# Feed-forward of a transformer block: gate and up products by seven 256-token blocks (Strassen) in place of eight, weight sums on GpSimd, down products a phase later

## The chip, the cores and the metric

The kernel runs on one core of a Trainium2 chip. The time is device time in microseconds of one launch, the median of several runs. A core has TensorE (PE in the profile), VectorE (DVE), ScalarE (ACT), GpSimd (POOL) and SyncE (SP), which issues the loads. Each engine works through its own queue in order; engines wait for each other on semaphores only.

## The reference

Two blocks of a language model in float32 over 512 tokens of width 1024. The first has two layers (a recurrent mixer and a sparse attention), each followed by the same feed-forward; the second has a retention and window attention mixer and a mixture of experts. Only the feed-forward matters here. It runs twice:

```python
D_FF = -(-8 * D_MODEL // (3 * 256)) * 256          # 2816

def swiglu(h, w_gu, w_down):
    u = h @ w_gu
    g, v = u[..., :D_FF], u[..., D_FF:]
    return (jax.nn.silu(g) * v) @ w_down
...
        h = h + swiglu(rmsnorm(h, norm_g[layer, 1]), ffn_w_gu[layer], ffn_w_down[layer])
```

## The kernel before

Float32 products are made of three matmuls each: every operand is split into a rounded part `hi` (ACT, a copy with another type) and the rest `lo` (DVE, a subtraction), and `three` multiplies hi by hi, hi by lo and lo by hi into one PSUM bank.

The hidden width 2816 is cut into 22 tiles of 128. Tokens are the moving operand. For one tile, `linear` makes the gate product into `bank[2v]` and the up product into `bank[2v+1]` (v is the tile's parity), each over eight slices of the model width, with 512 tokens at a time: 2 x 8 x 3 = 48 matmuls. The normalization's factor per token (`rn`) is multiplied in afterwards, twice on DVE (before and after the silu on ACT); DVE then multiplies gate by up into `hid`, ACT and DVE split it. `down` takes two hidden tiles (f = 0, 1) at once: for each half of the model width (hb = 0, 1) four output tiles into banks 4 to 7, first the four products of f = 0, then the four of f = 1, 48 matmuls in all. DVE's `add_y` adds each bank into `h`; a bank's first product of the next half waits for that add (`y_free`).

A pair of tiles is one trip of a hardware loop on each engine: on TensorE `linear`, `linear`, `down`. The order of the work on DVE and ACT is written out by hand in `ffn_pair` (lines near 1690 and 2390). Weight panels of 1 MB (gate and up columns of a tile) come into `a_raw[0]` and `a_raw[1]` in turn. SP's `load_a` (near line 535) waits for `a_ready` to show that DVE's `low_a` of the tile two before is done, as that is the last reader of the buffer. `load_b` does the same for the down weights, and both are issued from one queue in the order a0, b0, a1, b1. GpSimd does nothing in the feed-forward but sums of squares ahead of it.

## Time and profile before

| | us |
|---|---|
| median of 3 runs | 2142.63 |
| lowest and highest | 2141.57, 2142.84 |
| the profiled execution, from first to last instruction (span) | 2139.6 |
| TensorE busy | 2097.5 (98%) |
| DVE busy | 1267.3 (59%) |
| ACT busy | 836.2 (39%) |
| GpSimd busy | 270.8 (13%) |

The span is the profiled execution's own time between its first and last instruction. What a run takes outside it is not in the profile; the median of the runs is 3.0 us above the span. Busy times of an engine are the union of its instructions; matmuls overlap each other, so the time between two starts says more than the duration of one. The first feed-forward takes about 240 to 610 us of the span, the second about 1040 to 1400 us.

### The profile page before, as it was taken

To read this page: it belongs to the slowest core of one execution; us is meant where nothing else is said; L and a number is where in the kernel's file an instruction comes from. 1 tells how busy PE (TensorE), PEld (TensorE's weight loads), DVE (VectorE), ACT (ScalarE), POOL (GpSimd) and SP (SyncE) were. 2 spreads that over 40 slices of the span, in tenths; PEclk is the share of its full clock that TensorE was granted. 3 is DMA by queue.
4 is the path that set the end of the run, shared out by engine and by line. 5 is a ranking of instruction groups with operands and counts; after the bars stand their busy time and mean duration, and the time that the engine had idled before them with its cause. 6 is when DMAs were issued, how large, how long until landed. Compare 5 with 4: busy or idle time off the path is not lost.

```text
span 2139.6 us, 27223 instructions
## 1 busy us (share of the span) xinstructions
PE 2097.5 (98%) x10474; PEld 1579.8 (74%) x10474; DVE 1267.3 (59%) x1704; ACT 836.2 (39%) x1258; POOL 270.8 (13%) x234
## 2 busy tenths in 40 slices
PE   8999999999999999999999999999999999999998
PEld 6787788888878877888888888877778884333346
DVE  7887855554587678875655555488775454000038
ACT  6556522222253444774422222264542232222143
POOL 1334200000010064000100000020000023222220
PEclk9999999999999999999999999999999999999999
DMA  5322322223214352122322222212122158999961
GB/s 202 125 94 74 118 92 105 88 88 117 79 64 147 130 172 79 31 46 90 131 91 99 104 88 88 98 61 78 60 99 98 62 239 321 418 408 401 391 238 60
DMA packets 62622, 298.13 MB, mean 139 GB/s; under 512 B 14080, under 2 KB 14464, under 8 KB 34582
## 3 DMA queue, kind: packets, MB, share of 16 engines
q1 hardware_dynamic: 42560, 261.60, 32.0%
q0 software_dynamic: 19552, 34.55, 5.3%
q8 instruction: 63, 1.03, 0.2%
q10 hardware_dynamic: 416, 0.70, 0.1%
q14 instruction: 31, 0.25, 0.0%
HBM read 326.37 MB, written 22.48 MB: 163 GB/s over the span
## 4 chain that ended last, share of the span: by engine, by line
PE 80%; DVE 8%; DMA 5%; ACT 3%; issue 2%; POOL 1%; POOLq 0%; ACTq 0%; DVEq 0%
PE psum L652 21%; PE psum L654 21%; PE psum L653 21%; PE psum L1413 5%; PE psum L1437 3%; DMA panel<-w_m 3%; PE psum L1102 2%; PE psum L1077 1%; DVE a_lo L2137 1%; DMA over_panel<-w_m,over_row 1%; ACT a_hi L1520 1%; DVE xc L2294 1%; DVE hs L2248 1%; ACT hn_hi L1547 0%; PE psum L1235 0%
## 5 line engine op out<-in xcount | busy, mean ns | idle before, releaser
L652 PE MATMUL psum<-hn_hi,a_hi 128*128 128x512 f32 (+1 forms) x1592 | 628.2, 395 | 1.9 <-DVE a_lo L2126 0.9
L654 PE MATMUL psum<-hn_hi,a_lo 128*128 128x512 f32 (+1 forms) x1592 | 618.5, 389 | 0.0
L653 PE MATMUL psum<-hn_lo,a_hi 128*128 128x512 f32 (+1 forms) x1592 | 618.1, 388 | 0.0
L652 PEld LDWEIGHTS psum<-hn_hi,a_hi 128*128 128x128 f32 (+1 forms) x1592 | 297.0, 187 | 73.5 <-issue 7.8
L653 PEld LDWEIGHTS psum<-hn_lo,a_hi 128*128 128x128 f32 (+1 forms) x1592 | 297.1, 187 | 64.8 <-issue 2.4
L654 PEld LDWEIGHTS psum<-hn_hi,a_lo 128*128 128x128 f32 (+1 forms) x1592 | 297.0, 187 | 64.4
L2137 DVE TENSOR_TENSOR a_lo<-a_raw,a_hi 128x2048 fp32r<-128x2048 f32 (+2 forms) x108 | 247.2, 2289 | 69.6 <-ACT a_hi L1520 69.1
L1520 ACT ACTIVATE a_hi<-a_raw 128x2048 fp32r<-128x2048 f32 (+2 forms) x108 | 201.3, 1866 | 71.2 <-PE psum L654 62.0
L2236 DVE TENSOR_TENSOR h<-h,psum 128x512 f32<-128x512 f32 x176 | 119.4, 686 | 78.4 <-PE psum L654 78.4
L3150 POOL TENSOR_TENSOR sq<-sq 128x512 f32<-128x512 f32 x5 | 7.8, 1555 | 1118.2 <-ACT sq L1533 1118.2
L3072 DVE TENSOR_TENSOR xhid<-xsg,psum 128x256 f32<-128x256 f32 x24 | 10.1, 421 | 232.3 <-ACT xsg L2081 232.3
L1701 ACT ACTIVATE sg<-sg 128x512 f32<-128x512 f32 x44 | 27.8, 632 | 286.2 <-DVE sg L2407 286.2
L652 PE MATMUL psum<-hid_hi,b_hi 128*128 128x512 f32 x352 | 137.3, 390 | 2.1 <-DVE h L2236 2.0
L654 PE MATMUL psum<-hid_hi,b_lo 128*128 128x512 f32 x352 | 137.0, 389 | 0.0
L653 PE MATMUL psum<-hid_lo,b_hi 128*128 128x512 f32 x352 | 136.9, 389 | 0.0
L1413 PE MATMUL psum<-panel,xw 128*64 128x512 f32 x512 | 113.4, 595 | 0.0
L2412 DVE TENSOR_TENSOR hid<-sg,psum 128x512 f32<-128x512 f32 x44 | 30.3, 688 | 113.8 <-PE psum L654 113.7
L1703 ACT ACTIVATE hid_hi<-hid 128x512 fp32r<-128x512 f32 x44 | 27.8, 632 | 177.5 <-DVE hid L2412 177.5
L1527 ACT ACTIVATE b_hi<-b_raw 128x1024 fp32r<-128x1024 f32 x64 | 66.9, 1050 | 65.5 <-PE psum L654 63.2
L1413 PEld LDWEIGHTS psum<-panel,xw 128*64 128x64 f32 x512 | 35.4, 137 | 66.8 <-issue 66.5
L2143 DVE TENSOR_TENSOR b_lo<-b_raw,b_hi 128x1024 fp32r<-128x1024 f32 x64 | 79.7, 1252 | 1.0 <-ACT b_hi L1527 1.0
L652 PEld LDWEIGHTS psum<-hid_hi,b_hi 128*128 128x128 f32 x352 | 66.1, 188 | 17.4 <-issue 2.6
(533 smaller groups left out, 3261.2 us busy)
## 6 DMA issues: line engine op xcount, KB each, us to landing
a_raw<-w_a SPq DMA_DIRECT2D x115, 1024.0 KB, 5.0
panel<-w_m SPq DMA_DIRECT2D x96, 1024.0 KB
b_raw<-w_b SPq DMA_DIRECT2D x64, 512.0 KB, 3.4
q_scratch<-q_hi POOLq DMA_DIRECT2D x7, 384.0 KB
q_scratch<-qb_lo POOLq DMA_DIRECT2D x7, 384.0 KB
q_hi<-q_scratch POOLq DMA_DIRECT2D x7, 384.0 KB
q_lo<-q_scratch POOLq DMA_DIRECT2D x7, 384.0 KB
token_rows<-nat POOLq DMA_DIRECT2D x4, 512.0 KB, 5.5
```

The costliest lines, as they stand in the source:

```text
L652: pe.matmul(out, w_hi, x_hi, start=first, stop=False)
L653: pe.matmul(out, w_hi, x_lo, start=False, stop=False)
L654: return pe.matmul(out, w_lo, x_hi, start=False, stop=last)
L1102: mm = pe.matmul(bank[6 + at % 2][side * DV:(side + 1) * DV, t * P:(t + 1) * P], w, x, start=i == 0, stop=i == len(steps) - 1)
L1413: mm = pe.matmul(bank[v][rows, :], xw[:, v, k, rows], w[half][:, k % 4 * 2 * EFF:(k % 4 + 1) * 2 * EFF], start=k == 0, stop=k == KT - 1)
L1437: mm = pe.matmul(bank[4 + 2 * v + hb][rows, :], xturn[:, v, f * P + half * SLOTS:f * P + (half + 1) * SLOTS], w[half][:, f * D + hb * 512: ...
L1520: act.activation(a_hi[s % 2][:, 0:w], a_raw[s % 2][:, 0:w], ACT.Copy).then_inc(a_rounded, 1)
L1527: act.activation(b_hi[s % 2][:, :], b_raw[s % 2][:, :], ACT.Copy).then_inc(b_rounded, 1)
L2137: V.tensor_tensor(a_lo[s % 2][:, 0:w], a_raw[s % 2][:, 0:w], a_hi[s % 2][:, 0:w], ALU.subtract) \
L2143: V.tensor_tensor(b_lo[s % 2][:, :], b_raw[s % 2][:, :], b_hi[s % 2][:, :], ALU.subtract) \
L2236: V.tensor_tensor(h[:, m, :], h[:, m, :], bank[4 + m % 4][:, :], ALU.add).then_inc(y_free, 1)
L2412: V.tensor_tensor(hid[:, f, :], sg[:, f, :], ps[1][:, :], ALU.mult).then_inc(tile_free, 2)
```

## The change

For 20 of a feed-forward's 22 tiles (all but the first two) gate and up are made together as a 2 by 2 block product by Strassen's method in Winograd's form. The blocks are: the two halves of the model width (four slices each), gate or up columns, and tokens 0 to 255 or 256 to 511. Seven block products of 4 slices x 3 matmuls with 256 columns take the place of eight: `P_1, P_2, P_6, P_7, P_5` in the tile's own phase, `P_3` and `P_4` in the phase of the tile after. Each has its own weight slot (`slot_hi`, `slot_lo`), one buffer each.

Four weight sums a tile (`S_1` to `S_4`, 128x512) and the second scaling of the gate are made on GpSimd, which holds them in one buffer `wsum`. Four token transforms (`T1` to `T4`, of the normalized input with its gain, for each of four slices) are made once in front, on ACT, GpSimd, ACT and DVE. Partial results are copied from PSUM by ACT (`copy_1` to `copy_3`) and added by DVE (`add_11`, `add_21`, `add_22`). The splitting of a tile's weights, one 2048-wide instruction on ACT and one on DVE before, becomes five on each: `high_1`/`low_1` and `high_s23`/`low_s23` 1024 wide, `s1`, `s4` and `a22` 512 wide. `a_ready` is now counted up by `low_a22`. SP's code is unchanged. `down` of a pair stands between the two phases of the next pair, and the loop's bounds change with it. The tables `rel` and `dk`, loaded by GpSimd ahead of the second feed-forward before, are loaded behind it.

The core of the diff, in the order TensorE, ACT, DVE, GpSimd (what is left out are index helpers, buffer declarations and the small functions whose names say what they read, round or add):

```diff
+            def seven(out, slot, x_hi, x_lo, again=False):
+                for k in range(KT // 2):
+                    mm = three(out, slot_hi[:, slot, k, :], slot_lo[:, slot, k, :], x_hi(k), x_lo(k),
+                               not again and k == 0, k == KT // 2 - 1, again)
+                return mm
+            def tx(n):
+                return lambda k: tx_hi[:, k, n, :], lambda k: tx_lo[:, k, n, :]
+            def hn_block(k0, c):
+                return lambda k: hn_hi[:, k0 + k, c], lambda k: hn_lo[:, k0 + k, c]
+            def fast_phase(sa, g, i, v):
+                n, m = sa + v + 2 * i, v - 2 + 2 * i
+                first = isinstance(i, int) and m == 0
+                x, z, y = bank[2 * v][:, 0:HALF], bank[2 * v + 1][:, 0:HALF], bank[2 * v + 1][:, HALF:S]
+                split, copied = split_at(g) + 4 * m, copied_at(g) + 3 * m
+                pe.wait_ge(tile_free, 2 * n - 2)
+                pe.wait_ge(w_split, split + 1)
+                seven(x, P_1, *hn_block(0, slice(0, HALF))).then_inc(w_used, 1)
+                seven(y, P_2, *hn_block(KT // 2, slice(0, HALF))).then_inc(w_used, 1)
+                if not first:
+                    pe.wait_ge(part_copied, copied)
+                    pe.wait_ge(w_split, split + 2)
+                    seven(bank[2 - 2 * v][:, 0:HALF], P_3, *hn_block(KT // 2, slice(HALF, S)), again=True) \
+                        .then_inc(w_used, 1)
+                else:
+                    pe.wait_ge(tx_ready, tx_at(g + 1))
+                pe.wait_ge(part_copied, copied + 1)
+                pe.wait_ge(w_split, split + 3)
+                seven(x, P_6, *tx(T2), again=True).then_inc(w_used, 2 if first else 1)
+                if not first:
+                    pe.wait_ge(a_ready, n)
+                    pe.wait_ge(part_added, added_at(g) + 2 * m)
+                    seven(bank[3 - 2 * v][:, 0:HALF], P_4, *tx(T4), again=True).then_inc(tile_ready, 2)
+                pe.wait_ge(part_added, added_at(g) + 2 * m + 1)
+                seven(z, P_7, *tx(T3)).then_inc(w_used, 1)
+                pe.wait_ge(part_copied, copied + 2)
+                pe.wait_ge(w_split, split + 4)
+                seven(x, P_5, *tx(T1), again=True).then_inc(w_used, 1)
...
+            def ffn(sa, sb_, e, trips, q, t, g):
                 linear_first(sa, q)
                 sums(t)
                 linear(sa + 1)
+                fast_phase(sa, g, 1, 0)
                 down(sb_, e, 0, hid_hi, hid_lo, P)
-                with pe.Fori(1, trips) as i:
-                    linear(sa, i)
-                    linear(sa + 1, i)
-                    down(sb_, e, i, hid_hi, hid_lo, P)
-
-            ffn(A_FF0, B_FF0, E_FF0, FF_TILES // 2, N_FFN0, T_FFN0)
+                fast_phase(sa, g, 1, 1)
+                with pe.Fori(2, trips) as i:
+                    fast_phase(sa, g, i, 0)
+                    down(sb_ - 2, e - 1, i, hid_hi, hid_lo, P)
+                    fast_phase(sa, g, i, 1)
+                fast_last(sa, g)
+                down(sb_, e, trips - 1, hid_hi, hid_lo, P)
...
+            def high_tx(g, k):
+                act.wait_ge(tx_made, tx_at(g, 4) + 4 * k + 4)
+                act.activation(tx_hi[:, k, :, :], tx_of(k), ACT.Copy).then_inc(tx_rounded, 1)
...
+            def first_pair(sa, sb_, e, t, g, gain):
+                gain_x(0, gain)
+                high_a(sa + 1)
+                gain_x(1, gain)
+                gain_x(2, gain)
+                high_tx(g, 0)
+                high_b(sb_)
+                act.wait_ge(tx_ready, tx_at(g) + 1)
+                gain_x(3, gain)
+                high_tx(g, 1)
+                high_b(sb_ + 1)
+                high_tx(g, 2)
+                root_wide(t)
+                high_1(sa, g, 1, 0)
+                high_tx(g, 3)
+                silu(e, 0, 0)
+                high_hid(0, tile_free, 2 * sa + 2)
+                high_s23(sa, g, 1, 0)
+                high_s1(sa, g, 1, 0)
+
+            def fast_pair(sa, sb_, e, i, g, last=False):
+                first = isinstance(i, int) and i == 1
+                copy_1(g, i, 0)
+                high_1(sa, g, i, 1)
+                silu(e, i - 1, 1)
+                copy_2(sa, g, i, 0)
+                high_s4(g, 2 * i - 1)
+                high_hid(1, *((tile_free, 2 * sa + 4) if first else (hid_made, hid_at(g) - 2 + 2 * i)))
+                high_a22(sa, i, 0)
+                high_s23(sa, g, i, 1)
+                copy_3(g, i, 0)
+                high_s1(sa, g, i, 1)
+                high_b(sb_, i)
+                copy_1(g, i, 1)
+                high_b(sb_ + 1, i)
+                if not last:
+                    high_1(sa, g, i + 1, 0)
+                silu(e, i, 0)
+                copy_2(sa, g, i, 1)
+                high_s4(g, 2 * i)
+                high_hid(0, hid_made, hid_at(g) - 1 + 2 * i)
+                high_a22(sa, i, 1)
+                if not last:
+                    high_s23(sa, g, i + 1, 0)
+                copy_3(g, i, 1)
+                if not last:
+                    high_s1(sa, g, i + 1, 0)
+
+            def ffn(sa, sb_, e, trips, t, g, gain):
+                first_pair(sa, sb_, e, t, g, gain)
+                fast_pair(sa, sb_, e, 1, g)
+                with act.Fori(2, trips - 1) as i:
+                    fast_pair(sa, sb_, e, i, g)
+                fast_pair(sa, sb_, e, trips - 1, g, last=True)
+                act.wait_ge(w_used, used_at(g + 1) - 2)
...
+            def low_a22(n, v):
+                V.wait_ge(a_rounded, n + 1)
+                V.tensor_tensor(slot_lo[:, P_4, :, :], panel_view(v)[:, KT // 2:KT, 1, :], slot_hi[:, P_4, :, :], ALU.subtract) \
+                 .then_inc(a_ready, 1)
...
+            def first_pair(sa, sb_, e, t, g):
+                low_a(sa + 1)
+                low_tx(g, 0)
+                low_b(sb_)
+                low_tx(g, 1)
+                low_b(sb_ + 1)
+                low_tx(g, 2)
+                inverse_wide(t)
+                gate(e, sa, 0, 0)
+                low_1(g, 0, 0)
+                low_tx(g, 3)
+                hidden(e, sa, 0)
+                low_hid(e, 0, 0)
+                low_s23(g, 0, first=True)
+                gate(e, sa + 1, 0, 1)
+                low_s1(g, 0)
+
+            def fast_pair(sa, sb_, e, i, g, last=False):
+                first = isinstance(i, int) and i == 1
+                n, m = sa + 2 * i, 2 * i - 2
+                add_11(g, m, 0)
+                if first:
+                    hidden(e, sa + 1, 1)
+                low_1(g, m + 1, 1)
+                scale_11(g, m, 0)
+                if not first:
+                    scale_12(used_at(g) + 6 * m + 3, 1)
+                low_s4(split_at(g) + 4 * m + 6)
+                if not first:
+                    add_21(n - 1, 1)
+                    fast_hidden(e, n - 1, i - 1, 1)
+                low_hid(e, i - 1, 1)
+                low_a22(n, 0)
+                low_s23(g, m + 1)
+                add_22(g, m, 0)
+                low_s1(g, m + 1)
+                for k in range(4):
+                    add_y(sb_ - 2 + 2 * i, k)
+                low_b(sb_, i)
+                for k in range(4, KT):
+                    add_y(sb_ - 2 + 2 * i, k)
+                add_11(g, m + 1, 1)
+                low_b(sb_ + 1, i)
+                scale_11(g, m + 1, 1)
+                if not last:
+                    low_1(g, m + 2, 0)
+                scale_12(used_at(g) + 6 * m + 9, 0)
+                low_s4(split_at(g) + 4 * m + (9 if last else 10))
+                add_21(n, 0)
+                fast_hidden(e, n, i, 0)
+                low_hid(e, i, 0)
+                low_a22(n + 1, 1)
+                if not last:
+                    low_s23(g, m + 2)
+                add_22(g, m + 1, 1)
+                if not last:
+                    low_s1(g, m + 2)
...
+            def make_tx(g, k):
+                x, tx = x_of(k), tx_of(k)
+                b11, b12, b21, b22 = x[:, 0, 0:HALF], x[:, 0, HALF:S], x[:, 1, 0:HALF], x[:, 1, HALF:S]
+                pool.wait_ge(x_gained, gained_at(g) + 2 * k + 2)
+                pool.tensor_tensor(tx[:, T1, :], b12, b11, ALU.subtract).then_inc(tx_made, 1)
+                pool.tensor_tensor(tx[:, T3, :], b22, b12, ALU.subtract).then_inc(tx_made, 1)
+                pool.wait_ge(tx_made, tx_at(g, 4) + 4 * k + 1)
+                pool.tensor_tensor(tx[:, T2, :], b22, tx[:, T1, :], ALU.subtract).then_inc(tx_made, 1)
+                pool.wait_ge(tx_made, tx_at(g, 4) + 4 * k + 3)
+                pool.tensor_tensor(tx[:, T4, :], b21, tx[:, T2, :], ALU.subtract).then_inc(tx_made, 1)
+            def sum_three(sa, g, i, v):
+                m, first = v - 2 + 2 * i, isinstance(i, int) and v - 2 + 2 * i == 0
+                a, done = panel_view(v), summed_at(g) + 4 * m
+                pool.wait_ge(a_loaded[(sa + v) % 2], 16 * ((sa + v) // 2 + i) + 16)
+                if first:
+                    pool.wait_ge(tx_ready, tx_at(g + 1))
+                else:
+                    pool.wait_ge(w_split, split_at(g) + 4 * m)
+                pool.tensor_tensor(wsum[:, S_1, :, :], a[:, 0:4, 1, :], a[:, 4:8, 1, :], ALU.add).then_inc(w_summed, 1)
+                pool.tensor_tensor(wsum[:, S_3, :, :], a[:, 0:4, 0, :], a[:, 0:4, 1, :], ALU.subtract).then_inc(w_summed, 1)
+                pool.wait_ge(w_summed, done + 1)
+                pool.tensor_tensor(wsum[:, S_2, :, :], wsum[:, S_1, :, :], a[:, 0:4, 0, :], ALU.subtract) \
+                    .then_inc(w_summed, 1)
+            def sum_last(g, i, v):
+                m, first = v - 2 + 2 * i, isinstance(i, int) and v - 2 + 2 * i == 0
+                pool.wait_ge(w_summed, summed_at(g) + 4 * m + 3)
+                if not first:
+                    pool.wait_ge(w_split, split_at(g) + 4 * m + 2)
+                pool.tensor_tensor(wsum[:, S_4, :, :], panel_view(v)[:, 4:8, 0, :], wsum[:, S_2, :, :], ALU.subtract) \
+                    .then_inc(w_summed, 1)
+            def scale_gate(e, i, v):
+                pool.wait_ge(gate_done, 2 * (e - E_FF0 + i) + v + 1)
+                pool.tensor_tensor(sg[:, v, :], sg[:, v, :], rn[:, :], ALU.mult).then_inc(gate_scaled, 1)
+            def fast_pair(sa, e, i, g, last=False):
+                if not (isinstance(i, int) and i == 1):
+                    scale_gate(e, i - 1, 1)
+                sum_three(sa, g, i, 1)
+                sum_last(g, i, 1)
+                if not last:
+                    sum_three(sa, g, i + 1, 0)
+                scale_gate(e, i, 0)
+                if not last:
+                    sum_last(g, i + 1, 0)
+            def ffn(sa, e, trips, g):
+                for k in range(KT // 2):
+                    make_tx(g, k)
+                sum_three(sa, g, 1, 0)
+                sum_last(g, 1, 0)
+                fast_pair(sa, e, 1, g)
+                with pool.Fori(2, trips - 1) as i:
+                    fast_pair(sa, e, i, g)
+                fast_pair(sa, e, trips - 1, g, last=True)
+                scale_gate(e, trips - 1, 1)
```

## Rows read from the trace of the kernel before

**Rows 1.** The page: engine totals, and the chain of waits by engine.

```profile
PE 2097.5 (98%) x10474; PEld 1579.8 (74%) x10474; DVE 1267.3 (59%) x1704; ACT 836.2 (39%) x1258; POOL 270.8 (13%) x234
...
PE 80%; DVE 8%; DMA 5%; ACT 3%; issue 2%; POOL 1%; POOLq 0%; ACTq 0%; DVEq 0%
```

**Rows 2.** Busy time by engine in one pair and in nearly ten (us, instructions in brackets).

```profile
310.00:342.64 32.64, 32.64 (x145) 27.04 (x144) 17.65 (x20) 8.15 (x8) 0.00 (x0) 1.00 0.26 96
280.00:600.00 320.00, 320.00 (x1414) 265.05 (x1413) 173.01 (x195) 80.10 (x80) 0.00 (x0) 1.00 0.26 95
```

**Rows 3.** Timeline of TensorE, 512 columns (start us, us, engine, line).

```profile
317.72 0.39 PE L652 MATMUL psum<-hn_hi,a_hi 128*128 128x512 f32 x1
317.95 0.39 PE L653 MATMUL psum<-hn_lo,a_hi 128*128 128x512 f32 x1
...
318.85 0.39 PE L654 MATMUL psum<-hn_hi,a_lo 128*128 128x512 f32 x1
```

**Rows 4.** Timeline of TensorE, 256 columns, and a weight load there.

```profile
2125.26 0.28 PE L652 MATMUL psum<-hn_hi,a_hi 128*128 128x256 f32 x1
2125.38 0.28 PE L653 MATMUL psum<-hn_lo,a_hi 128*128 128x256 f32 x1
...
2125.26 0.19 PEld L653 LDWEIGHTS psum<-hn_lo,a_hi 128*128 128x128 f32 x1
```

**Rows 5.** Instructions by shape (busy us, mean ns); last GpSimd's min/median/max ns.

```profile
L3072 DVE TENSOR_TENSOR xhid<-xsg,psum 128x256 f32<-128x256 f32 x24 | 10.1, 421 | 232.3 <-ACT xsg L2081 232.3
L2414 DVE TENSOR_TENSOR hid_lo<-hid,hid_hi 128x512 fp32r<-128x512 f32 x44 | 30.5, 692 | 30.7 <-ACT hid_hi L1703 30.7
L2143 DVE TENSOR_TENSOR b_lo<-b_raw,b_hi 128x1024 fp32r<-128x1024 f32 x38 | 46.2, 1218 | 0.0
...
L2081 ACT ACTIVATE xsg<-psum 128x256 f32<-128x256 f32 x24 | 9.2, 384 | 139.6 <-PE psum L1413 133.4 <-issue 6.1
L1703 ACT ACTIVATE hid_hi<-hid 128x512 fp32r<-128x512 f32 x44 | 27.8, 632 | 177.5 <-DVE hid L2412 177.5
L1527 ACT ACTIVATE b_hi<-b_raw 128x1024 fp32r<-128x1024 f32 x64 | 66.9, 1050 | 65.5 <-PE psum L654 63.2 <-DMA b_raw<-w_b 2.2
...
L3150 POOL TENSOR_TENSOR sq<-sq,tmp x10: 1292/1558/3157, 242.4 to 1728.6; 128x512 f32<-128x512 f32 x10
```

**Rows 6.** Timelines of GpSimd and DVE where they overlap.

```profile
1717.40 2.40 POOL L3150 TENSOR_TENSOR sq<-sq 128x512 f32<-128x512 f32 x1 [302.26 <-ACT sq L1533]
1727.15 4.64 POOL L3150 TENSOR_TENSOR sq<-sq,tmp 128x512 f32<-128x512 f32 x2 [7.34 <-ACT tmp L1533]
...
1718.58 0.68 DVE L2681 TENSOR_TENSOR h<-h,psum 128x512 f32<-128x512 f32 x1
1727.25 3.39 DVE L2137 TENSOR_TENSOR a_lo<-a_raw,a_hi 128x2048 fp32r<-128x2048 f32 x1
```

**Rows 7.** Timeline of DVE in the feed-forward loop.

```profile
319.37 0.69 DVE L2407 TENSOR_TENSOR sg<-psum,rn 128x512 f32<-128x512 f32 x1 [1.50 <-PE psum L654]
320.76 0.69 DVE L2409 TENSOR_TENSOR sg<-sg,rn 128x512 f32<-128x512 f32 x1 [0.70 <-ACT sg L1701]
...
327.98 2.29 DVE L2137 TENSOR_TENSOR a_lo<-a_raw,a_hi 128x2048 fp32r<-128x2048 f32 x1 [1.11 <-ACT a_hi L1520]
```

**Rows 8.** DMA issues of the page: the panels (KB each, median us to landing).

```profile
a_raw<-w_a SPq DMA_DIRECT2D x115, 1024.0 KB, 5.0
```

**Rows 9.** Timelines around the first feed-forward's prologue.

```profile
258.94 3.35 DVE L2169 RECIPROCAL rn<-rn 128x512 f32<-128x512 f32 x1 [3.03 <-ACT rn L1544]
...
268.91 0.39 PE L652 MATMUL psum<-hid_hi,b_hi 128*128 128x512 f32 x1
```

**Rows 10.** Windows in the experts' stage; PEclk is the granted clock.

```profile
1894.00:1898.00 4.00, 3.18 (x8) 1.14 (x10) 0.43 (x1) 0.11 (x1) 0.00 (x0) 0.64 1.02 411
1940.00:1966.00 26.00, 25.13 (x118) 8.06 (x113) 2.55 (x6) 5.65 (x10) 6.03 (x6) 1.00 1.02 410
```

**Rows 11.** The chain that ended last, in order of time (start us, us, what).

```profile
1878.53 16.16 DMA panel<-w_m
```

More of the change, by code:

```diff
@@ L28 @@
 FF_TILES = 2816 // P
+HALF = S // 2
+T1, T2, T3, T4 = range(4)
+S_2, S_3, S_1, S_4 = range(4)
+P_1, P_2, P_6, P_7, P_5, P_3, P_4 = range(7)
+NFAST = FF_TILES - 2
 HEADS, GROUPS, DQK, DV = 16, 4, 96, 64
@@ L3171, in _ @@
             sums(T_FFN0)
+            ffn(A_FF0, E_FF0, FF_TILES // 2, 0)
             sums(T_KV)
```

265 lines of the change are left out of this document (194 added, 71 removed).

## The prediction

> **What bounds the kernel now.** I read the page's engine totals and chain first: TensorE is busy 98% of the span and four fifths of the chain of waits is TensorE [rows 1]. The stretch 280 to 600 us, nearly ten pairs of feed-forward tiles, has TensorE busy 320.00 of 320.00 us, DVE 173, ACT 80 and GpSimd nothing; one pair lasts 32.64 us and DVE works 17.65 of it [rows 2]. So here only fewer or shorter matmuls can gain, and other work is free as long as no matmul waits for it. The reader is to see how much room DVE has before and who will want it.
>
> **The products.** A matmul of 512 columns starts 0.2267 us after the one before it (317.72 to 317.95; over the pair's 144, 32.64 us) [rows 2, 3]. One of 256 columns, with the same kinds of operand, starts 0.12 us after (2125.26 to 2125.38), although a weight load lasts 0.19 us; the loads overlap [rows 4]. Gate and up of a tile are 2x8x3 = 48 matmuls now, 48 x 0.2267 = 10.88 us; seven products are 7x4x3 = 84, 84 x 0.12 = 10.08 us. That is 0.80 us a tile, 20 fast tiles in each of two feed-forwards: -32.0 us. A pair without any wait: 32.64 - 1.6 = 31.04 us, in the order first tile's phase A 0 to 10.08 (seven groups of 1.44: 1, 2, 3', 6, 4', 7, 5; a prime is the tile before), down products 10.08 to 20.96, phase B of the second tile 20.96 to 31.04.
>
> **What the other engines get.** Per tile, by width: DVE 256 wide x5 (0.42 us), 512 wide x5 (0.69), 1024 wide x3 (1.22, the old b_lo included), and four adds into h (0.69, as the other 512 wide) [rows 5]: 2.1 + 3.5 + 3.7 + 2.8 = 12.0 us, 24 us a pair where it was 17.65. Queued ones start 0.09 earlier, about 21 us. ACT: 3x0.38 + 5x0.63 + 3x1.05 = 7.4, 15 us a pair, no bound. GpSimd: four sums and the gate scaling, 5 a tile. Its 512-wide TENSOR_TENSOR takes 1.29 us at the least, 1.56 in the median, waits for DVE included [rows 5]: 12.9 us a pair. No row shows these sums' strided reading; I take 1.29, with 1.56 as upper end; as lower end the 0.69 of DVE's instruction of that width.
>
> **GpSimd beside DVE.** At 1727.15 GpSimd starts two 512-wide operations and at 1727.25 DVE a 2048-wide subtraction of two SBUF tensors. DVE takes 3.39 in place of 2.29 [rows 7], GpSimd 4.64 in place of 2.6: exactly what comes out if one waits for the other's whole instruction, GpSimd 1727.15 to 1728.45, DVE to 1730.64, GpSimd to 1731.8. At 1717.40 it is GpSimd that waits, 2.40 in all. The add from PSUM at 1718.58 takes 0.68 beside GpSimd's, undisturbed [rows 6]. Of the new DVE work only add_11, scale_12, add_21, add_22 and the h adds read PSUM. The rest, 9 instructions a tile, about 7.5 us, shares one turn with GpSimd's 6.5: 14 of the 15.5 us of a tile's share, and in turns.
> The Trainium skill, SBUF — State Buffer, "SBUF: two separate sides", says the same: an exclusive lock between GpSimd and a DVE instruction with two SBUF inputs, held for the whole instruction. By that rule, the trace agrees (3.39 against 2.29 us). A reader who took it as shared bandwidth would price case 2 below.
>
> **The queues, worked through for pairs 2 to 10.** Hops: a product's end reaches DVE or ACT 0.29 us after its last slot (last matmul 318.85, next slot 319.08, DVE 319.37); DVE to ACT to DVE costs 0.07 beside the work (319.37 to 320.76) [rows 3, 7]. A panel lands 5.0 us after its issue (median of 115) [rows 8], and SP issues about 0.15 after the DVE instruction that frees the buffer.
> Phase B, from its start: product 2 done 3.17; ACT's high_1 to 4.22; DVE low_b 3.5 to 4.7, scale_11, low_1 5.0 to 6.2, scale_12 to 6.5; silu to 7.2; GpSimd scale_gate 7.2 to 8.5; low_s4, which waits for it, to 9.2; GpSimd's last sum 9.2 to 10.5; fast_hidden to 11.2; high_hid to 11.85; low_hid to 12.5; low_a22 to 13.15. No matmul of phase B waits (copy_2 is done at 7.5, product 5 wants it at 8.64). But this runs 3.1 us into the next pair (t = 0 is its start), and four waits follow:
> (a) copy_3 stands in ACT's queue behind high_hid, high_a22 and high_s23: done t = 3.55, product 3' wants it at 2.88: **0.7 us**.
> (b) SP's load of the second tile's panel waits for a_ready, now given by low_a22 at 3.1: issued 3.25, landed 8.25. Behind it: high_1 to 9.35, low_1 to 10.6, scale_11, scale_12 to 11.3, silu to 11.95, copy_2 to 12.3 (ACT takes silu first). Product 5, due at 8.64 + 0.7, starts at 12.3: **2.95 us**. Before the change no product waits for a panel: TensorE has no gap in 320 us [rows 2].
> (c) GpSimd and DVE then take turns: scale_gate to 13.3, low_s4 14.0, sum 15.2, fast_hidden 15.9, sum 17.1, low_hid 17.8 (high_hid between). Down products begin at 13.8; four groups of the first hidden half cover 2.7 us, then they wait for low_hid: **1.3 us**.
> (d) low_s23 and low_s1 of the next tile stand before the eight h adds in DVE's queue, and low_s23 waits for GpSimd's third sum: sum 19.0, low_a22, last sum 20.9, low_s23 22.1 (high_s23 20.1), add_22, low_s1 23.0, first add into h 23.6. Down's second half wants the bank that this add frees at 20.6: **3.1 us**.
> 8.05 us a pair: 31.04 + 8.05 = 39.1 against 32.64, **+6.5 us** for each of 9 pairs: +58.5.
> **First pair and prologue:** -1.6 for the tiles. In front of it, ACT's root_wide (behind it now DVE's reciprocal from 258.94, 3.35 us, and the first down product at 268.91 [rows 9]) stands behind eight gains, three rounded transforms, and those behind 12 GpSimd operations of 256 columns. No row has that width: between half of 1.29 and 1.29; I take 0.75, 9 us, plus about 3 of turns with a_lo and b_lo. The reciprocal ends about 267.8, low_1 and low_tx go before hidden, the banks come free at about 271.6 where TensorE wants them at 268.9: 2.7. The first three weight sums start only when all transforms are split (270.6), low_s23 ends 277.2, product 6 wanted it 2.4 earlier; product 7 another 0.4. **+5.5** (bounds 1 to 12 by the two widths).
> **End:** after the last phase B product 3' wants copy_3 at once, 2.4 us early; then the last hidden half comes 0.8 after down's first half ends. **+3.2** (0 to 5).
> Code outside the loops (the two table loads moved behind the second feed-forward, used 50 us later) costs nothing.
>
> **Sum.** Per feed-forward 58.5 - 1.6 + 5.5 + 3.2 = 65.6; two: +131. The span is 2139.6 and the median of the runs lies 3.0 above it: 2139.6 + 131 + 3.0 = **2274 us**.
>
> **The rivals.**
> 2. No turns: GpSimd fits into DVE's gaps. Phase B's chain then ends at 11.75, (a) goes, the panel lands at 6.85, copy_2 ends 10.85: (b) 2.2, (c) 0; the three sums run 11.9 to 15.8 and the first add ends 19.8 against 17.8: (d) 2.0. Period 35.3, +2.6 x 9 = 23.6, and 3 and 2 us at the ends: +27 each, **2197**. For it: DVE has 7 us of idle and PSUM work a pair; against it rows 6. 20%, partial turns between 2197 and 2274 included.
> 3. Longer: GpSimd's strided sums at 1.54 (+0.25 x 7 in the chain, x 18 = 31), **2305**. A half clock would end there too: at 1894 to 1898, after a wait of 16 us on a panel, the granted clock is 0.64, but over 1940 to 1966 of the same stage 1.00 [rows 10, 11]; one spell of half clock a pair, 1.7 us x 18, is +31. The Trainium skill, TensorE: Matmul & The Clock Gate, "What's actually happening", has the clock fall to 1.2 GHz after idling; my gaps of 3 us are shorter than that row's, so I give it a few per cent. Together 18%.
> 4. Faster: the chain keeps ahead of TensorE. It decides at two points: the second panel must land by t = 4.6 (copy_2 by 8.64), and the first add into h must be done 5.4 us after down starts. Then -32 and some 5 us at each prologue: **2120**. For it, every engine's sum of work is under 31 us; against it, low_a22 comes behind product 4' of phase B (ends 7.2), so even with nothing queued the panel lands after 5.5. 9%.
> 5. Something within 0.2% (4 us, about what a measurement here tells from no change): waits of 1.6 us a pair, no mechanism gives them; 2%.
> The forecast itself has 49%, the remainder of 2% lies above 2320. Faster 0.10, same 0.02, slower 0.88. The range takes in cases 1 to 3: 2190 to 2320.
>
> **What would show it.** In the changed profile: groups of twelve 256-column matmuls 1.44 us long; a pair of 39 us; TensorE at a loop's pair busy about four fifths; its waits named copy_2 (ACT pc2), hid_lo and h (DVE) in that order of place, with 3, 1.3 and 3 us; a_raw's issues right behind the low_a22 subtraction, high_1 waiting for the DMA; two-SBUF DVE instructions lasting up to 1.3 us longer than rows 5. GpSimd's operations at twice 1.29 in the middle of a pair. I am wrong in (b) if ACT's high_1 of the second tile doesn't wait for a panel, in (d) if the first h add of a pair starts with its y product, and altogether if the pair lasts under 34 us.

## The result, and the profile after

| | us |
|---|---|
| after, median of 4 runs | 2271.76 |
| lowest and highest | 2268.63, 2275.22 |
| before, median of 4 runs beside them | 2142.74 |
| ratio, 95% interval | 1.0607 (1.0592 to 1.0623) |
| the profiled execution after: its time, its span | 2268.63, 2266.6 |

The change costs 129 us; the forecast was +131, 2274 us, range 2190 to 2320. The page's totals, the three TensorE groups with most idle time before them, and the panels' loads; the first line is to be read beside [rows 1]:

```profile
PE 2108.1 (93%) x11914; PEld 1642.2 (72%) x11914; DVE 1463.2 (65%) x1992; ACT 961.3 (42%) x1562; POOL 613.8 (27%) x466
...
L720 PE MATMUL psum<-tx_hi,slot_hi 128*128 128x256 f32 x640 | 187.5, 293 | 48.2 <-ACT pc L1875 46.2
L720 PE MATMUL psum<-hid_hi,b_hi 128*128 128x512 f32 x352 | 146.5, 416 | 44.8 <-DVE h L2467 36.3
L720 PE MATMUL psum<-hn_hi,slot_hi 128*128 128x256 f32 x480 | 139.6, 291 | 24.0 <-DVE hid L2637 15.6
...
a_raw<-w_a SPq DMA_DIRECT2D x115, 1024.0 KB, 4.8
```

TensorE is busy 93% in place of 98%. These three groups hold 117 us of idle time. In the first it is mostly product 5, which waits for ACT's copy_2 (`pc`, L1875); in the second the down products, which wait for the adds into `h` and for `hid_lo`; in the third mostly the first fast phase of each feed-forward, which waits for DVE's `hid` (L2637).

Two pairs of the loop, as in [rows 2] (after the window's length come the busy times of PE, PEld, DVE, ACT and GpSimd, each with its instructions, then the granted clock, the DMA share and GB/s). Behind them the four waits of one pair on TensorE's timeline:

```profile
393.50:431.60 38.10, 32.20 (x218) 29.10 (x218) 26.91 (x34) 13.39 (x23) 15.29 (x10) 1.00 0.23 82
431.60:469.70 38.10, 33.40 (x217) 30.29 (x217) 27.00 (x34) 13.51 (x23) 15.29 (x10) 0.96 0.23 83
```

```profile
388.30 0.38 PE L720 MATMUL psum<-hn_hi,slot_hi 128*128 128x256 f32 x1 [0.36 <-ACT pc L1882]
...
396.90 0.38 PE L720 MATMUL psum<-tx_hi,slot_hi 128*128 128x256 f32 x1 [2.60 <-ACT pc L1875]
...
401.87 0.50 PE L720 MATMUL psum<-hid_hi,b_hi 128*128 128x512 f32 x1 [0.52 <-DVE hid_lo L2641]
407.33 0.50 PE L720 MATMUL psum<-hid_hi,b_hi 128*128 128x512 f32 x1 [2.41 <-DVE h L2467]
```

From the start of one pair's down products to the next is 38.0 us on average over nine intervals of the first feed-forward (285.03 to 626.79), 38.2 in the second, where it was 32.64. The four waits are (a) to (d) of the forecast, in its order.

Wait (b) in the next pair, on the timeline of all engines: low_a22 (L2656) frees the buffer, SP issues the load, ACT's high_1 (L1834) waits for it to land, and low_1, scale_12, silu and copy_2 stand one behind the other up to product 5.

```profile
425.18 0.69 DVE L2656 TENSOR_TENSOR slot_lo<-a_raw,slot_hi 128x512 fp32r<-128x512 f32 x1
426.04 0.33 SPq L608 DMA_DIRECT2D a_raw<-w_a  x1
...
431.02 1.06 ACT L1834 ACTIVATE slot_hi<-a_raw 128x1024 fp32r<-128x1024 f32 x1 [3.95 <-DMA a_raw<-w_a]
432.12 1.23 DVE L2645 TENSOR_TENSOR slot_lo<-a_raw,slot_hi 128x1024 fp32r<-128x1024 f32 x1 [3.58 <-ACT slot_hi L1834]
433.59 0.42 DVE L2680 TENSOR_TENSOR sg<-psum,rn 128x256 f32<-128x256 f32 x1
434.04 0.63 ACT L1822 ACTIVATE sg<-sg 128x512 f32<-128x512 f32 x1 [1.96 <-DVE sg L2680]
434.58 0.36 ACT L1875 ACTIVATE pc<-psum 128x256 f32<-128x256 f32 x1
435.07 0.38 PE L720 MATMUL psum<-tx_hi,slot_hi 128*128 128x256 f32 x1 [2.65 <-ACT pc L1875]
```

Wait (d), in the same pair (GpSimd's and DVE's timelines): GpSimd's sums, 1.29 us alone, last 1.73 to 1.75 us in turns with DVE, and the first add into `h` (L2467) stands behind low_s23 (L2661), which waits for the third sum.

```profile
437.68 1.74 POOL L3527 TENSOR_TENSOR wsum<-a_raw 128x512 f32<-128x512 f32 x1
439.37 1.75 POOL L3529 TENSOR_TENSOR wsum<-wsum,a_raw 128x512 f32<-128x512 f32 x1
...
438.96 1.00 DVE L2641 TENSOR_TENSOR hid_lo<-hid,hid_hi 128x512 fp32r<-128x512 f32 x1 [0.70 <-ACT hid_hi L1826]
439.89 1.78 DVE L2656 TENSOR_TENSOR slot_lo<-a_raw,slot_hi 128x512 fp32r<-128x512 f32 x1
442.33 1.58 DVE L2661 TENSOR_TENSOR slot_lo<-wsum,slot_hi 128x1024 fp32r<-128x1024 f32 x1 [0.66 <-ACT slot_hi L1854]
444.76 1.87 DVE L2467 TENSOR_TENSOR h<-h,psum 128x512 f32<-128x512 f32 x3
```

In front of the two feed-forwards (DVE, then TensorE), beside [rows 9]: the reciprocal starts 8 us later than before, and the first fast phases wait 6.1 and 9.5 us.

```profile
267.01 3.34 DVE L2400 RECIPROCAL rn<-rn 128x512 f32<-128x512 f32 x1
...
274.78 0.58 PE L720 MATMUL psum<-hn_hi,slot_hi 128*128 128x256 f32 x1 [6.14 <-DVE hid L2637]
...
1129.62 0.58 PE L720 MATMUL psum<-hn_hi,slot_hi 128*128 128x256 f32 x1 [9.51 <-DVE hid L2637]
```

### The profile page after: what moved, and what is told of

It is laid out like the page before. It is cut to its first block and busy times, and to the rows that moved or that the text cites. A ratio compares the mean times of both kernels' runs of the same rounds, so it can differ in the third digit from the quotient of the medians.

```text
span 2266.6 us, 31937 instructions
## 1 busy us (share of the span) xinstructions
PE 2108.1 (93%) x11914; PEld 1642.2 (72%) x11914; DVE 1463.2 (65%) x1992; ACT 961.3 (42%) x1562; POOL 613.8 (27%) x466
## 5 line engine op out<-in xcount | busy, mean ns | idle before, releaser
L720 PE MATMUL psum<-hn_hi,a_hi 128*128 128x512 f32 (+2 forms) x952 | 379.2, 398 | 1.9 <-DVE a_lo L2357 0.9
L722 PE MATMUL psum<-hn_hi,a_lo 128*128 128x512 f32 (+2 forms) x952 | 369.5, 388 | 0.0
L721 PE MATMUL psum<-hn_lo,a_hi 128*128 128x512 f32 (+2 forms) x952 | 369.2, 388 | 0.0
L720 PE MATMUL psum<-tx_hi,slot_hi 128*128 128x256 f32 x640 | 187.5, 293 | 48.2 <-ACT pc L1875 46.2
L2368 DVE TENSOR_TENSOR a_lo<-a_raw,a_hi 128x2048 fp32r<-128x2048 f32 (+3 forms) x68 | 157.2, 2312 | 47.8 <-ACT a_hi L1642 47.3
L722 PE MATMUL psum<-tx_hi,slot_lo 128*128 128x256 f32 x640 | 185.7, 290 | 0.0
L721 PE MATMUL psum<-tx_lo,slot_hi 128*128 128x256 f32 x640 | 185.5, 290 | 0.0
L720 PE MATMUL psum<-hn_hi,slot_hi 128*128 128x256 f32 x480 | 139.6, 291 | 24.0 <-DVE hid L2637 15.6
L721 PE MATMUL psum<-hn_lo,slot_hi 128*128 128x256 f32 x480 | 137.3, 286 | 0.0
L722 PE MATMUL psum<-hn_hi,slot_lo 128*128 128x256 f32 x480 | 137.1, 286 | 0.0
```

What stands on the lines that cost most here:

```text
L720: pe.matmul(out, w_hi, x_hi, start=first, stop=False, skip_group_check=again)
L721: pe.matmul(out, w_hi, x_lo, start=False, stop=False, skip_group_check=again)
L722: return pe.matmul(out, w_lo, x_hi, start=False, stop=last, skip_group_check=again)
L2368: V.tensor_tensor(a_lo[s % 2][:, 0:w], a_raw[s % 2][:, 0:w], a_hi[s % 2][:, 0:w], ALU.subtract) \
```

## The experiments

The theory is the forecast's: the matmuls are 0.8 us a tile shorter, and queue order, one late panel load and turns between GpSimd and DVE add four waits a pair. The rivals: that DVE's and GpSimd's load sets the pair whatever the order; that the products are not shorter; that the length of GpSimd's sums counts, not the turns. e1 to e5 are edits of the changed kernel; e6 and e7 build on e5, each later one on the one before. "Pair" is the mean over the same nine intervals as above. "Second feed-forward done" is when its last down matmul starts in the profiled execution. What follows it is the same code in every kernel after the change, yet it took 736.7 to 745.2 us, so a few us between two totals need not come from the edit; this column leaves them out. Ratios are to runs of the kernel before, taken beside each. e3, e4 and e7 compute other values than the reference.

| kernel | pair | second feed-forward done | time, us | ratio to before |
|---|---|---|---|---|
| before | 32.64 | 1398.0 | 2142.7 | |
| after | 38.0 | 1524.7 | 2271.8 | 1.0607 |
| e1_adds_first | 35.9 | 1484.5 | 2229.3 | 1.0413 (1.0395 to 1.0430) |
| e2_early_panel | 34.0 | 1454.3 | 2200.4 | 1.0279 (1.0262 to 1.0296) |
| e3_sums_memset | 36.2 | 1490.5 | 2235.1, one run | |
| e4_sums_gone | 34.8 | 1460.8 | 2199.5, one run | |
| e5_both | 31.3 | 1400.5 | 2143.5 | 1.0012 (1.0003 to 1.0021) |
| e6_prologue | | 1400.6 | 2148.7 | 1.0040 (1.0026 to 1.0054) |
| e7_split | | 1395.3 | 2135.2 | 0.9967 (0.9956 to 0.9978) |
| e8_front | | 1397.8 | 2142.8 | 1.0003 (0.9994 to 1.0012) |
| e9_order | | 1392.7 | 2134.8 | 0.9973 (0.9962 to 0.9984) |
| e9_order_pool | | 1395.2 | 2136.8 | 0.9979 (0.9969 to 0.9988) |

### e1_adds_first: wait (d) alone

```diff
                 low_a22(n, 0)
+                for k in range(4):
+                    add_y(sb_ - 2 + 2 * i, k)
                 low_s23(g, m + 1)
                 add_22(g, m, 0)
                 low_s1(g, m + 1)
-                for k in range(4):
-                    add_y(sb_ - 2 + 2 * i, k)
```

> One edit to the kernel after the change: DVE's first four adds into h stand ahead of low_s23, add_22 and low_s1 in its queue. Theory (wait d is a matter of queue order): the first add no longer waits for GpSimd's third sum and high_s23, starts about 3 us earlier, and TensorE's wait on h in the middle of the down products (2.6 us a pair in the changed kernel's trace) goes. A pair takes 35.5 us in place of 38.1, the kernel 2222 us (2205 to 2240). Rival A (DVE's and GpSimd's load in turns sets the pair, not the order): the wait moves to another place, a pair stays within 0.5 us of 38.1 and the kernel above 2260. Rival B (low_s23, now 2.8 us later, becomes late for product 6 of phase B): a new wait there of 1 to 2 us, kernel 2235 to 2255.

2229.3 us, inside the range. The group of down products has no wait on `h` left (first row below), and nothing new appears at product 6, so both rivals are out: moving four adds forward is enough to take (d) away. The pair is 35.9 us in place of the expected 35.5. (b) stays, and behind it come stretches in which the granted clock is half; the two intervals without one take 35.3 and 35.6 us (last section).

```profile
L720 PE MATMUL psum<-hid_hi,b_hi 128*128 128x512 f32 x352 | 145.6, 414 | 7.9 <-DVE hid_lo L2641 7.9
...
425.94 0.38 PE L720 MATMUL psum<-tx_hi,slot_hi 128*128 128x256 f32 x1 [2.53 <-ACT pc L1875]
```

### e2_early_panel: wait (b) alone

```diff
-            slot_hi = sb("slot_hi", [P, 7, KT // 2, P], F32R, st)
+            slot_hi = sb("slot_hi", [P, 8, KT // 2, P], F32R, st)
...
                 high_b(sb_, i)
+                high_a22(sa, i, 1)
...
                 low_b(sb_, i)
+                low_a22(n + 1, 1, summed_at(g) + 4 * m + 8)
```

(`slot_lo` likewise. The second tile's product 4 reads the eighth slot, and its old high_a22 and low_a22 are gone. The third argument of low_a22 is a wait for the sums, which read the panel too.)

> One edit to the kernel after the change: the weight slot of product 4 is there twice, so that high_a22 and low_a22 of the second tile stand half a pair earlier in the queues and the next panel's load starts then. Theory (wait b is the panel's load released late, and the chain behind it carries c and most of d): high_1 of the second tile no longer waits for a DMA, TensorE's 2.75 us in front of product 5 go, the chain of silu, gate scaling, hidden tile comes about 4 us earlier against 2.75 for TensorE, so that c goes and d loses 1 us or more. A pair takes 34.5 us in place of 38.1, the kernel 2200 us (2180 to 2230). Rival A (load in turns sets the pair): high_1 finds its panel, and still the pair takes over 37.5 us, kernel above 2258. Rival B (the load is only as late as its neighbours, product 5 then waits for DVE's low_1 instead): b falls to 1.5, pair 36.5, kernel 2238.

2200.4 us: as expected, with (a) and (c) gone too, and a pair even 0.5 us shorter than expected. But (d) did not lose the 1 us that I gave it; this row of TensorE's stands in every pair:

```profile
429.45 0.50 PE L720 MATMUL psum<-hid_hi,b_hi 128*128 128x512 f32 x1 [2.46 <-DVE h L2467]
```

I read it so, without a run of its own: a late panel holds TensorE and DVE's chain back together, so removing (b) brings both forward by the same time.

### e3_sums_memset and e4_sums_gone: what GpSimd costs, and how

```diff
+            def fill(slot, r):
...
+                pool.memset(wsum[:, slot, :, 1:P], 0.0)
...
+                    pool.memset(flat[:, 0:740], 0.0).then_inc(w_summed, 1)
...
-                pool.tensor_tensor(wsum[:, S_1, :, :], a[:, 0:4, 1, :], a[:, 4:8, 1, :], ALU.add).then_inc(w_summed, 1)
+                pool.tensor_tensor(wsum[:, S_1, :, 0:1], a[:, 0:4, 1, 0:1], a[:, 4:8, 1, 0:1], ALU.add)
+                fill(S_1, 0)
```

(This is e3, and so for the other sums; e4 has the addition of one column a slice alone.)

> Left out: the weight sums. In place of each of GpSimd's four sums a tile stand an addition of one column a slice and fills of the same destination and of idle buffers, about 1.25 us together, which read no SBUF tensor. Everything that waits for a sum waits as before. Theory (GpSimd and DVE wait for each other's whole instructions): DVE's subtractions beside the fills take their undisturbed 0.69 and 1.22 us, the pair falls to about 35.5 us (my second rival's 35.3), the kernel to 2220 (2200 to 2240). Rival A (the length of GpSimd's chain counts, not the turns): pair within 0.7 us of 38.1, kernel above 2255. Rival C (the lock holds for any GpSimd access of SBUF, fills too): the fills and DVE's instructions are stretched as the sums were and nothing changes.

> Left out: the weight sums but for one column a slice (0.1 to 0.2 us each). Theory: what stays are waits a and b, which come from queue order and the panel's load: b about 2.2 us, c none, d under 0.5; pair 34.0 us, kernel 2190 (2170 to 2210). Rival (TensorE's own 256-column matmuls or the clock, not waits): pair above 36. Rival (GpSimd's sums cost it all): pair at 31.3, kernel 2140 or under.

DVE's groups in the changed kernel and then in e3, where GpSimd works as long (1.28 us from one sum's start to the next, undisturbed) but reads four columns a sum:

```profile
L2661 DVE TENSOR_TENSOR slot_lo<-wsum,slot_hi 128x1024 fp32r<-128x1024 f32 x40 | 55.5, 1389 | 19.6 <-ACT slot_hi L1854 19.6
L2693 DVE TENSOR_TENSOR hid<-sg,up 128x512 f32<-128x512 f32 x40 | 52.7, 1319 | 7.4 <-POOL sg L3542 3.5
L2656 DVE TENSOR_TENSOR slot_lo<-a_raw,slot_hi 128x512 fp32r<-128x512 f32 x40 | 49.2, 1229 | 0.0
```

```profile
L2661 DVE TENSOR_TENSOR slot_lo<-wsum,slot_hi 128x1024 fp32r<-128x1024 f32 x40 | 49.0, 1225 | 40.9 <-ACT slot_hi L1854 40.9
L2656 DVE TENSOR_TENSOR slot_lo<-a_raw,slot_hi 128x512 fp32r<-128x512 f32 x40 | 28.1, 703 | 0.0
L2693 DVE TENSOR_TENSOR hid<-sg,up 128x512 f32<-128x512 f32 x40 | 27.7, 692 | 7.4 <-POOL sg L3553 3.5
...
L3525 POOL MEMSET tmp<- 128x740 f32 x80 | 57.4, 718 | 0.0
```

low_a22 and the product into `hid` fall from 1.23 and 1.32 us to 0.70 and 0.69, the undisturbed time of [rows 5]: the turns are with GpSimd's reading, and a fill takes none, so rival C is out. The Trainium skill, SBUF — State Buffer, "SBUF: two separate sides", has a DVE instruction with two SBUF inputs locked out only by a GpSimd one that reads SBUF; by that rule, the trace agrees (0.69 beside fills, 1.32 beside sums). But these turns are worth 34 to 37 us of the kernel (1524.7 - 1490.5 in the profiles, 2271.8 - 2235.1 in the totals), not the 77 between my forecast and rival 2. That is a lower bound: the short sums still take turns (L3537's last 0.54 us in the mean, 0.21 undisturbed). e3's expected 2220 was 15 us too fast. (c) is gone in e3 and (d) is 0.5 to 2.1 us, so both had turns in them; rival A, the length of GpSimd's chain alone, is out.

e4 took 2199.5 us in place of the expected 2190, a pair 34.8 in place of 34.0: (b) is still 2.3 to 2.65 us of idle time with no sums to wait for, where I expected 2.2, and some intervals have a stretch of half clock (up to 36.2 us; those without one take 34.5 to 34.7). The sums, turns and length together, cost 64 us up to the end of the second feed-forward (1524.7 - 1460.8); that e4's total is 72 us lower has its other 8 us elsewhere, 5 of them behind the feed-forwards. "The sums cost it all" falls, and so does "it is the matmuls". And (d) is under 0.5 us here, with the adds in their old place: it took the order and the sums together to make it, and either edit removes it.

### e5_both: both edits of the loop

> The edits of e1 and e2 together: second slot for product 4 with its panel's load half a pair earlier, and the first four adds into h ahead of low_s23. Theory (a pair is 31.04 us of products plus the waits that queue order makes, and the two edits remove b and d): e2's only wait over 0.5 us in a pair (2.6 on h) goes, with it 0.3 us of small ones; a pair takes 31.3 us in place of e2's 34.0, 18 pairs and the first of each feed-forward give 51 us: 2149 us (2140 to 2160), slower than before by what the two prologues still cost. Rival A (DVE and GpSimd together can't do a pair's work in 31 us): the pair stays above 32.6, kernel above 2172. Rival B (the products themselves are not 0.8 us a tile shorter in the loop): no wait over 0.5 us is left in a pair and it still takes over 32.

2143.5 us. One window as long as a pair was after the change, then two groups of TensorE and one of DVE:

```profile
393.50:431.60 38.10, 38.10 (x275) 36.03 (x275) 31.59 (x43) 16.26 (x27) 17.31 (x13) 1.00 0.35 122
```

```profile
L720 PE MATMUL psum<-tx_hi,slot_hi 128*128 128x256 f32 x640 | 181.3, 283 | 1.1 <-DVE slot_lo L2663 1.1
L720 PE MATMUL psum<-hid_hi,b_hi 128*128 128x512 f32 x352 | 140.2, 398 | 5.8 <-DVE hid_lo L2641 5.8
...
L2658 DVE TENSOR_TENSOR slot_lo<-a_raw,slot_hi 128x512 fp32r<-128x512 f32 x40 | 67.8, 1696 | 0.0
```

TensorE has no idle time in that window, and from the second interval on a pair lasts 31.2 to 31.3 us (31.04 forecast without waits), 1.4 less than before. DVE's low_a22 is stretched to 1.70 us by GpSimd, more than ever, and nobody waits for it: the same turns cost nothing once the chain has slack. The rivals of load and of products that aren't shorter are both out. Some 98 us of the 129 were lost in the loop, and one edit of order and one more slot give them back and 23 us more. What keeps e5 from beating the kernel before is what stands ahead of the loops and behind them.

### e6_prologue: the front, first order

The down products of pair 0 come before the first fast phase, the reciprocal before the second transform, and two transforms use other buffers (ACT's queue):

```diff
                 high_b(sb_)
+                root_wide(t)
+                gain_x(2, gain)
...
                 high_tx(g, 2)
-                root_wide(t)
```

> e5 with another order ahead of the loop: root_wide and inverse_wide before the second token transform, the first pair's down products before the first fast phase (as in the kernel before), the temporaries of two transforms in other buffers, so that the first hidden tile need not wait for them. Theory (a wait of 6.1 us ahead of the first fast phase comes from the reciprocal's place behind GpSimd's twelve transforms, and with it the spell of half clock and the 1.4 us at product 6): some 8 us less a feed-forward, 2133 us (2120 to 2145), faster than before. Rival A (GpSimd's transforms and sums in front are the bound, wherever the reciprocal stands): the wait moves to product 6 of the first fast phases and e6 is within 4 us of e5. Rival B (two fast phases without down products between them starve, as DVE and GpSimd have 10 us a tile there and need more): a new wait of 3 us or more in front of the second phase's product 6 or 7, e6 2140 to 2150.

2148.7 us in place of the expected 2133: a miss. The wait of 6.1 us went (1.3 us stay in its place, 4.8 in the second feed-forward), and 4.1 us on hid_lo came in the middle of the first down products, 3.4 us on copy_2 in the second fast phase (TensorE):

```profile
277.11 0.50 PE L722 MATMUL psum<-hid_hi,b_hi 128*128 128x512 f32 x1 [4.13 <-DVE hid_lo L2650]
...
306.40 0.39 PE L722 MATMUL psum<-tx_hi,slot_hi 128*128 128x256 f32 x1 [3.35 <-ACT pc L1877]
```

Up to the end of the second feed-forward e6 is level with e5 (1400.6 and 1400.5 us): what one place gained another lost. The 5 us between their totals aren't in the feed-forwards as profiled. Rival A's "within 4 us of e5" holds by the profiles, but its wait at product 6 did not come. Rival B had the place right (two fast phases in a row) and the time, though the late piece there was copy_2, in front of product 5, not product 6 or 7.

### e7_split: the down products inside the first phase

```diff
-                fast_phase(sa, g, 1, 0)
+                fast_head(sa, g)        # products 1 and 2
                 down(sb_, e, 0, hid_hi, hid_lo, P)
+                fast_tail(sa, g)        # products 6, 7 and 5
```

Products 2 and 7 of this phase have each other's half bank here, so gate and up of one tile in each feed-forward are not the reference's. The part behind the feed-forwards takes 3.9 us less than in e9_order, which computes the right values; whether the values are why was not tried. So read this time from the feed-forwards.

> e5 (second slot for product 4, adds first) with e6's early reciprocal and temporaries, and the first pair's down products between products 1 and 2 of the first fast phase and its products 6, 7 and 5; the first low_a22 and copy_1 come before the second half of these down products. Theory (the waits in front are 6.1 and 9.5 us in e5 because the reciprocal stands behind the transforms, and e6 lost the gain again because hidden tile 1 and, later, the panel freed by low_a22 were late): TensorE starts product 1 some 9 and 12 us earlier, hidden tile 1 is ready before the down products want it or within 1 us, the sums have 10 us more, and the wait of 3.35 us on copy_2 goes. 2125 us (2118 to 2134), faster than before. Rival (every order in front leaves 8 us or more of waits, as GpSimd's sixteen transforms and four sums take 25 us with their turns whatever stands beside them): product 6 or hidden tile 1 waits over 4 us, 2138 us or more.

Better than e5 by 5.2 us at the end of the second feed-forward, under a third of the 18 expected: the first down products still wait 2.8 us for hid_lo (1.6 in the second feed-forward), and product 5 of the second phase 2.9 us for copy_2. Neither the theory's waits of under 1 us nor the rival's of over 4 came.

### e8_front: gate of tile 1 first, down weights' splits later

This is DVE's queue in front. In the second fast phase low_b moves from before scale_11 to behind scale_12 and fast_hidden, and low_a22 to behind scale_12.

```diff
                 inverse_wide(t)
                 gate(e, sa, 0, 0)
                 low_tx(g, 1)
-                hidden(e, sa, 0)
                 low_1(g, 0, 0)
+                hidden(e, sa, 0)
+                gate(e, sa + 1, 0, 1)
+                low_b(sb_)
```

> e7 with products 2 and 7 of the first fast phase in each other's half bank as they belong (e7 had them exchanged, which changes no duration), and a third order in front: root_wide and inverse_wide first of all behind the first transform, the gate of tile 1 ahead of the transforms' and weights' subtractions, and, in the second fast phase, the splits of the down weights behind scale_12. Theory (what e7 still waits in front, 2.8 us on hid_lo with a spell of half clock behind it and 3.2 us on copy_2 in the first feed-forward, 3.1, 1.6 and 3.2 us in the second, is DVE's order again): at most 1.5 us on each of the two remains, 2123 us (2117 to 2129). Rival (DVE's and ACT's work in front is too much, some 30 us of it between the norm and the first hidden tile, in whatever order): the waits move on to the next consumer, low_1 or a b panel, and the time stays within 3 us of e7's 2135.

2142.8 us in place of the expected 2123: a miss, and the most instructive one. The waits in the first down products are gone, but moving low_b behind scale_12 moved more than a subtraction. SP, ACT and TensorE:

```profile
303.15 0.33 SPq L618 DMA_DIRECT2D b_raw<-w_b  x1
303.68 0.33 SPq L610 DMA_DIRECT2D a_raw<-w_a  x1
...
310.35 1.06 ACT L1855 ACTIVATE slot_hi<-a_raw 128x1024 fp32r<-128x1024 f32 x1 [5.82 <-DMA a_raw<-w_a]
...
314.40 0.58 PE L722 MATMUL psum<-tx_hi,slot_hi 128*128 128x256 f32 x1 [3.91 <-ACT pc L1896]
```

SP's b load waits for low_b, and the a load, whose buffer low_a22 had freed at 298.2, stands behind it in the one queue: 5.5 us later, wait (b) again.

### e9_order and e9_order_pool: the splits forward again

```diff
                 low_s1(g, 0)
+                low_b(sb_, 1)
                 low_1(g, 1, 1)
...
                 low_s4(split_at(g) + 4 * m + 6)
+                if first:
+                    low_b(sb_ + 1, i)
```

> e8 with the down weights' splits of the second pair moved forward again (the first one into the first pair's down products, the second behind low_s4): in e8 SP's load of a b panel stood in its queue until DVE's low_b was done at 303 us, and the next gate and up panel behind it, for which high_1 and then copy_2 waited (3.9 us and a spell of half clock, 2.7 us and a spell in the second feed-forward). Theory (SP's one queue): these waits go, 5.6 and 4.3 us, and 1 us of the smaller ones; 2132 us (2127 to 2137). Rival (the second fast phase is held up by DVE's total in front, and the panel was late in any case): a wait of 2 us or more stays in front of product 5 or moves to product 6, time 2137 to 2143.

> As e9_order, and the subtraction low_tx of the last transform is made by GpSimd instead of DVE, so that the weight sums need not wait for DVE's queue. Theory (the first sums start 3 us earlier, at 273 instead of 276 us; low_s23 of the first two fast tiles comes as much earlier and the 0.4 to 0.9 us waits of the second fast phase go): 2130 us (2125 to 2135), 2 us under e9_order. Rival (the turns eat it: DVE's subtractions beside GpSimd's 2 us instruction start later and hidden tile 1 comes late): a new wait of 1 us or more on hid_lo in the first down products, equal to or above e9_order.

2134.8 us: 0.27% faster than before, the interval wholly under 1, the best version found, and inside the range about the 2132 expected. The waits of 3.9 and 2.7 us behind the a load are gone, so SP's queue was the cause. What stays are waits of 1 to 2 us in the second fast phase, on DVE and on copy_2 (TensorE):

```profile
291.48 0.36 PE L722 MATMUL psum<-hn_hi,slot_hi 128*128 128x256 f32 x1 [1.56 <-DVE slot_lo L2686]
294.84 0.35 PE L722 MATMUL psum<-tx_hi,slot_hi 128*128 128x256 f32 x1 [1.69 <-DVE slot_lo L2698]
300.90 0.38 PE L722 MATMUL psum<-tx_hi,slot_hi 128*128 128x256 f32 x1 [1.52 <-ACT pc L1896]
```

With the last transform's subtraction on GpSimd (e9_order_pool) the first down products wait 1.6 and 1.8 us for hid_lo, as the rival had it, and the 2130 us of its theory did not come. It is 2 us slower than e9_order; the runs of the two overlap (2135.0 to 2138.9 and 2134.3 to 2137.2).

## Why the prediction was right

**The products.** The forecast had 31.04 us a pair without waits; e5 shows 31.23. Right to 0.2 us.

**The loop's waits.** Predicted 0.7 + 2.95 + 1.3 + 3.1 = 8.05 us. Measured in the pair above, start to start less the ordinary spacing: 0.5 + 2.75 + 0.7 + 2.55 = 6.5. Places, names, order and causes are as written: e1 took (d) out, e2 (b) and with it (a) and (c), e5 all four, and in e3 (c) went with the turns. That (b) is the load released late was right to 0.2 us. (c) and (d) are the mis-sized terms, 0.6 us each: from the end of the gate's scaling to that of the last sum I had 7.6 us (t = 13.3 to 20.9), and it took 6.8 (436.03 to 442.83), as one sum and one DVE instruction in turn take 1.74 us, not the 1.9 I wrote out, nor the twice 1.29 that I named as a sign. [rows 6] had shown it: GpSimd's 4.64 us there are less than three whole instructions, 1.29 + 2.29 + 1.29 = 4.87, so "exactly" was too much said. And the turns are a smaller part of the waits than I made them, the order a larger one: "no turns" was too cheap at 2197, e3 has 2235.

**The fronts and ends.** Predicted +5.5 and +3.2 a feed-forward. The fronts took 9.3 and 12.8 us: the first down products start 16.5 and 20.0 us later against what came before them, 7.2 of it for the five products now ahead of them. Within it, the wait for the banks is 6.1 and 9.5 us where I had 2.7; product 6 waits 0.7 and 1.3 us where I had 2.4; and the matmuls behind the long wait run at half clock (0.50 over 274 to 278 us), which I had not counted. The ends are right: 3.3 us in e5 (from the tenth down products, at 567.2 us, to the last matmul of the eleventh, at 605.0, 37.8 us in place of 34.5), though most of it is the last hidden half (1.8 us of idle time) and little the wait on copy_3 (0.5), the other way round from the forecast. As to why the fronts are late: the reciprocal ends at 270.35, not at 267.8, as 12 GpSimd operations of 256 columns took 15.3 us (249.3 to 264.6), not 12: 0.74 us alone, as I took it, but those that meet a DVE subtraction last 1.2 to 2.7. And the second feed-forward is worse than the first (9.5 against 6.1 us), which I hadn't looked for: its transforms start 3.8 us ahead of the sum of squares' product on TensorE (1041.25 and 1045.00 in e5), those of the first 7.4 (249.46 and 256.87).

**The sum was right in part because two errors cancel.** Nine intervals of 38.0 and nine of 38.2 in place of 32.64 are +98 us where I had 117; what is outside them is 12.5 and 16.4 us (the two feed-forwards end 60.5 and a further 66.2 us later) where I had 7.1 each; 0.4 us come behind them. 98 + 29 = 127 us, the difference of the two spans (2266.6 - 2139.6); the medians differ by 129, as the profiled execution after was 3 us under its median. A reader should trust the mechanism, and the loop's price to a fifth; that the total came out within 2 us is luck.

**Longer, faster, same.** Rival 4 named its own two points, the panel by t = 4.6 and the first add 5.4 us after down starts; e5 meets both and has the loop that rival 4 described. It was not wrong as mechanics, only not this kernel.

## What to carry to other kernels

Where an engine is full, price a change by the queues of the others: write each out in order, mark what every instruction waits for, and ask at which time the first consumer wants it. A buffer's last reader is where its next load starts, and a queue that issues loads for two streams ties the second to the first (e8). In this kernel engine turns cost only in a chain without slack: a subtraction of 1.7 us where 0.7 would do was free in e5. So change the order first and the work second. And where one edit trades waits for others (e6), read the stage in the profile beside the total.
